# The causal mask and the exponential of a chunked state-space scan, set up on another engine

## The chip, the cores and the metric

The kernel is one launch on one core of a Trainium2 chip. The metric is the device time of that launch in microseconds (us). The version before takes 2398.5 us, the median of three runs (2398.19 to 2401.05).

## The reference, cut to what matters

One layer of a decoder, 1024 tokens wide and long: sparse attention beside a Mamba-2 scan, gated and merged, then a squared-ReLU MLP. The change lies in the scan, in the part that works within chunks of 128 tokens:

```python
a_cum = jnp.cumsum(dt * a, axis=2)                    # within a chunk of 128 tokens, per head
seg = a_t[..., :, None] - a_t[..., None, :]           # a_cum[l] - a_cum[s]
decay = jnp.exp(jnp.where(tril, seg, -jnp.inf))       # 0 where s > l
cb = jnp.einsum('bclgn,bcsgn->bcgls', cm, bm)
y_diag = jnp.einsum('bcgls,bcghls,bcsghp->bclghp', cb, decay, xdt)
```

There are 4 groups of 8 heads and 8 chunks, so the 128x128 matrix `cb` is made 32 times and `decay` (8 heads of 128x128) 32 times.

## The kernel before, in words

Every engine has its own program, in a fixed order written by hand; they meet only at semaphores. TensorE (PE) carries the big products. Each float32 operand is split into a high and a low part, so a product is three matmuls. GpSimd (POOL) splits the weights, SyncE (SP) loads them.

The scan runs group by group (`for g in range(NG)`), in the profile from about 831 us to 1305 us. The four groups begin their chunk loops near 831, 967, 1097 and 1228 us. In a group the function `segments(k)` on PE prepares chunk k. It makes `cb` in PSUM bank 7 (`mm(ps[:, 7, 0:P], b_fm, c_fm)`, two records), and then, for the 8 heads, eight "pick" matmuls of 128 columns in bf16. A pick takes one head's row of `a_cum` out of `seg_rows`, in three bf16 pieces, and spreads it over 128 partitions in banks 0 and 1. So bank 0 and 1 hold a_cum[l] for partition s and column l.

ScalarE (ACT) turns that into the decay. Eight instructions (L1502) compute relu(a_cum[s] - a_cum[l]), with `dta` as the copy of a_cum with its sign kept; one more of 1024 columns (L1506) computes exp(-that). The relu keeps the exponent from growing where s > l; it does not zero that half. VectorE (DVE) does: L1905 copies `cb` out of PSUM times the 0/1 triangle `tri` into `cb_sb`, and L1908 multiplies the eight 128x128 decay matrices by it, in place. PE then uses them as weights (`ps<-xdt,decay`).

`decay` has two buffers, `cb_sb` and the banks 0, 1 and 7 one each. PE's program in a group is: segments(0), a part of "fill" work, segments(1), another part, and then for k = 0 to 7: the products of chunk k (wait for `mix_ready` of chunk k), segments(k + 2), and some fill. Fill is an independent projection (the z of the next group, or in the last group a gate) that is cut into parts of 24 matmuls of 256 columns, or 12 of 512 in the last group; one or two such parts stand in an iteration, none in the last two of the last group. segments(k) waits twice: before `cb` for `cb_out` of chunk k - 1, which tells that bank 7 has been read, and before the picks for `decay_done` of chunk k - 1, which tells that banks 0 and 1 have been read. On DVE, `mix_in(k + 1)` (L1905 and L1908) stands ahead of the state and output steps of chunk k (L1922 to L1937), the last of which signals `y_ready`. On ACT, each chunk's decay is followed by `fill_evac` (L1382) and `squares_of` (L1490).

Ahead of the first chunk of a group ACT still copies out the last transposed tile (L1444).

Of the kernel before, what the change touches and what calls it, by code (L numbers as in the profile page):

```python
# [14 lines left out]
P = 128  # L15
F32 = mybir.dt.float32
F32R = mybir.dt.float32r
BF16 = mybir.dt.bfloat16
ALU = mybir.AluOpType
# [41 lines left out]
def hybrid_block(nc, x, c, ada_w, ada_b, norm_g, w_in, kv_norm_g, kidx_norm_g, w_uk, w_uv, conv_w, conv_b,  # L61
# [6 lines left out]
    NS = dt_bias.shape[1]  # L68
# [74 lines left out]
    tri = place("tri", [P, P], F32)  # L143
    future = place("future", [P, P], F32)
    vec_a = place("vec_a", [P, 112], F32)
    vec_b = place("vec_b", [P, 112], F32)
# [107 lines left out]
    with ctx:  # L254
# [291 lines left out]
        def _(pool):  # L546
            nc.gpsimd.memset(ones[:, :], 1.0).then_inc(const_made, 1)
            nc.gpsimd.memset(ident[:, :], 0.0).then_inc(const_made, 1)
            nc.gpsimd.memset(future[:, :], 0.0).then_inc(const_made, 1)
            pool.wait_ge(const_made, 3)  # L550

# [7 lines left out]
                                    base=0, pattern=[[-1, P]], channel_multiplier=1).then_inc(const_made, 1)  # L559
            pool.wait_ge(const_made, 6)  # L560
            nc.gpsimd.tensor_copy(ident_bf[:, :], ident[:, :]).then_inc(const_made, 1)
# [78 lines left out]
        def _(pe):  # L640
# [59 lines left out]

            pe.wait_ge(const_made, 7)
            pe.wait_ge(small_in, 16 * 6)
# [265 lines left out]
            for g in range(NG):  # L968
# [57 lines left out]
                def segments(k):  # L1026


                    if k >= 1:
                        pe.wait_ge(cb_out, g * NT + k)  # L1030
                    r = slice(k * P, k * P + P)
                    mm(ps[:, 7, 0:P], b_fm[:, r], c_fm[:, r], start=True, stop=True)
                    if k >= 1:
                        pe.wait_ge(decay_done, 2 * (g * NT + k) - 1)
                    i0 = k % 4 * HG
                    for j in range(2):
                        o = ps[:, j, :]
                        for h in range(4):
                            last = mm(o[:, h * P:(h + 1) * P],
                                      seg_pick[0:NR, i0 + 4 * j + h:i0 + 4 * j + h + 1].broadcast_to([NR, P]),  # L1040
                                      seg_rows[0:NR, 2 * g + k // 4, :], start=(h == 0), stop=(h == 3))
                    last.then_inc(seg_done, 1)
# [42 lines left out]

            pe.wait_ge(decay_done, 2 * NG * NT)
            pe.wait_ge(fill_out, NG * 8)
# [100 lines left out]
        def _(act):  # L1188
# [156 lines left out]
            nc.scalar.activation(acum[:, :, :].rearrange(flat), ps[:, 6, 0:NT * NS], ACT.Copy, scale=-1.0).then_inc(aend_out, 1)  # L1345
            nc.scalar.copy(dta[:, :, :].rearrange(flat), ps[:, 6, 0:NT * NS]).then_inc(aend_out, 1)
            nc.scalar.activation(ea[:, :, :].rearrange(flat), ps[:, 6, 0:NT * NS], ACT.Exp).then_inc(aend_out, 1)
# [55 lines left out]
            for g in range(NG):  # L1403
# [92 lines left out]
                for k in range(NT + 2):  # L1496
                    if k < NT:
                        act.wait_ge(seg_done, g * NT + (k + 1))
                        if k >= 2:
                            act.wait_ge(mix_done, g * NT + (k - 1))  # L1500
                        for h in range(HG):
                            ins = nc.scalar.activation(decay[k % 2][:, h, :], ps[:, h // 4, (h % 4) * P:(h % 4 + 1) * P], ACT.Relu,  # L1502
                                                       bias=dta[:, k, bass.ds(g * HG + h, 1)], scale=-1.0)
                        ins.then_inc(decay_done, 1)
                        act.wait_ge(decay_done, 2 * (g * NT + k) + 1)
                        nc.scalar.activation(decay[k % 2][:, :, :], decay[k % 2][:, :, :], ACT.Exp, scale=-1.0).then_inc(decay_done, 1)  # L1506
                    if k == 1:
                        fill_evac(g, 1 if g else 0)
                    for part in fill_parts(g, k - 2) if k >= 2 else ():
                        if part % 2:  # L1510
                            fill_evac(g, part // 2)
                    if g == NG - 1 and k >= NT - 1:
                        first_acts({NT - 1: (0, 1), NT: (2,), NT + 1: (3,)}[k])
                    if k >= 2:
                        squares_of(k - 2)
# [121 lines left out]
        def _(dve):  # L1637
# [184 lines left out]
            dve.wait_ge(last_spilled, 16 * 2)  # L1822
            dve.wait_ge(aend_out, 4)
            V.link(ve.tensor_tensor(dte[:, :, :].rearrange("p c h -> p (c h)"), ps[:, 7, 0:NT * NS],
# [44 lines left out]
            for g in range(NG):  # L1869
# [30 lines left out]
                def mix_in(k):  # L1900

                    dve.wait_ge(seg_done, g * NT + (k + 1))
                    if g or k:
                        dve.wait_ge(mix_ready, g * NT + k)
                    ve.tensor_tensor(cb_sb[:, :], ps[:, 7, 0:P], tri[:, :], ALU.mult).then_inc(cb_out, 1)  # L1905
                    dve.wait_ge(cb_out, g * NT + (k + 1))
                    dve.wait_ge(decay_done, 2 * (g * NT + k + 1))
                    ve.tensor_tensor(decay[k % 2][:, :, :], decay[k % 2][:, :, :],  # L1908
                                     cb_sb[:, :].rearrange("p (o l) -> p o l", o=1).broadcast_to([P, HG, P]), ALU.mult).then_inc(mix_ready, 1)
# [188 lines left out]
```

## Time and profile before

| | |
|---|---|
| median of three runs | 2398.5 us |
| the profiled execution, its own time | 2398.5 us |
| its span | 2396.6 us |
| PE busy | 2315.8 us (97%) |
| DVE busy | 1336.9 us (56%) |
| ACT busy | 751.0 us (31%) |
| POOL busy | 960.2 us (40%) |
| chain that ended last, by engine | PE 89%, DVE 6%, issue 2%, ACT 2% |

The span is 1.9 us shorter than the time of the same execution. In a row of the profile, L and a number is the line of the kernel (nearly all matmuls have L648, the helper's line), `out<-in` are the tensors, and `[idle before <-releaser]` says how long the engine stood still and what ended it. PE's records overlap, since matmuls are pipelined: the distance between two starts is what one costs.

### The profile page before, as it was taken

The page shows a single profiled execution, that of the slowest core. Times are in us where ns is not written, and L with a number is a line of the kernel's source. Part 1 is how long each engine was busy: PE and PEld are TensorE (multiplying, and loading weights), DVE is VectorE, ACT ScalarE, POOL GpSimd, SP SyncE. Part 2 cuts the span into 40 slices and gives each one's busy share as a digit, 9 for nine tenths or more (in the row PEclk, how much of TensorE's full clock was granted, in tenths as well). Part 3 has the DMA queues.
Part 4 walks back from the last instruction along what each step waited for, and adds up shares of the span by engine and source line. Part 5 has one row for each costly group of instructions (what it writes and reads, how often), then busy time and mean ns, then how long its engine had stood idle before and what let it go on. Part 6 is the DMA issues. An engine that isn't in the chain of part 4 may idle for free.

```text
span 2396.6 us, 31872 instructions
## 1 busy us (share of the span) xinstructions
PE 2315.8 (97%) x11958; PEld 1913.6 (80%) x11958; DVE 1336.9 (56%) x1988; ACT 751.0 (31%) x1363; POOL 960.2 (40%) x628
## 2 busy tenths in 40 slices
PE   3999999998999999999999999999999999999997
PEld 3977888885557998989887888899888888888886
DVE  4259999996657177685867545425522322322325
ACT  5144121005653244545466111025511112112112
POOL 1221333236672373654555334446333233233222
PEclk8999999999999999999999999999999999999999
DMA  7111452225652113141223354224211111111103
GB/s 276 36 36 39 147 189 90 88 97 163 209 164 80 36 63 132 45 145 45 86 104 140 141 176 141 99 95 167 80 48 41 53 53 35 53 53 43 45 35 79
DMA packets 144731, 230.28 MB, mean 96 GB/s; under 512 B 7956, under 2 KB 111732, under 8 KB 143604
## 3 DMA queue, kind: packets, MB, share of 16 engines
q1 hardware_dynamic: 119936, 166.11, 21.0%
q10 hardware_dynamic: 23684, 59.06, 6.4%
q0 software_dynamic: 1008, 3.67, 0.9%
q8 instruction: 73, 1.20, 0.2%
q14 instruction: 30, 0.25, 0.0%
HBM read 176.39 MB, written 52.43 MB: 95 GB/s over the span
## 4 chain that ended last, share of the span: by engine, by line
PE 89%; DVE 6%; issue 2%; ACT 2%; DMA 1%; ACTq 0%; DVEq 0%
PE ps L648 87%; DVE score L1731 2%; DVE probT L1814 1%; DVE mod_sum L1658 1%; PE ps L977 1%; PE ps L873 1%; PE ps L910 1%; DMA gate_d<-last_spill 0%; PE ps L696 0%; DMA acts_d<-decay 0%; ACT decay L1502 0%; DMA rows_b<-in_ssm_norm_g_dram 0%; DVE a_lo L1867 0%; DVE prob L1797 0%; DVE acc L1958 0%
## 5 line engine op out<-in xcount | busy, mean ns | idle before, releaser
L648 PE MATMUL ps<-a_hi,w_hi 128*128 128x512 f32 x1728 | 676.9, 392 | 2.0 <-DVE a_lo L1867 1.2
L648 PE MATMUL ps<-a_lo,w_hi 128*128 128x512 f32 x1728 | 672.8, 389 | 0.0
L576 POOL CAST w_hi<-raw 128x2048 fp32r<-128x2048 f32 x90 | 174.7, 1941 | 1180.6 <-issue 858.8
L648 PE MATMUL ps<-a_hi,w_lo 128*128 128x512 f32 x1728 | 543.0, 389 | 0.0
L580 POOL TENSOR_TENSOR w_lo<-raw,w_hi 128x512 fp32r<-128x512 f32 (+1 forms) x360 | 521.1, 1479 | 7.2
L2028 DVE TENSOR_TENSOR x_tm<-x_tm,ps 128x1024 f32<-128x1024 f32 x120 | 146.6, 1221 | 453.7 <-PE ps L648 453.1
L648 PEld LDWEIGHTS ps<-a_hi,w_hi 128*128 128x128 f32 x1728 | 324.5, 188 | 70.5 <-DVE a_lo L1867 2.0
L648 PEld LDWEIGHTS ps<-a_hi,w_lo 128*128 128x128 f32 x1728 | 324.4, 188 | 67.9
L648 PEld LDWEIGHTS ps<-a_lo,w_hi 128*128 128x128 f32 x1728 | 324.5, 188 | 66.2 <-issue 0.2
L648 PE MATMUL ps<-w_hi,a_hi 128*128 128x256 f32 (+1 forms) x896 | 259.2, 289 | 4.4 <-DVE a_lo L1867 2.7
L648 PE MATMUL ps<-w_lo,a_hi 128*128 128x256 f32 (+1 forms) x896 | 253.5, 283 | 0.0
L648 PE MATMUL ps<-w_hi,a_lo 128*128 128x256 f32 (+1 forms) x896 | 253.5, 283 | 0.0
L648 PE MATMUL ps<-w_lo,u_hi 128*128 128x512 f32 x512 | 204.3, 399 | 0.0
L1613 ACT ACTIVATE u_tmp<-ps 128x512 f32<-128x512 f32 x64 | 38.0, 594 | 522.7 <-PE ps L648 522.7
L648 PE MATMUL ps<-w_hi,u_hi 128*128 128x512 f32 x512 | 201.7, 394 | 0.0
L648 PE MATMUL ps<-w_hi,u_lo 128*128 128x512 f32 x512 | 200.7, 392 | 0.0
L648 PEld LDWEIGHTS ps<-w_hi,a_hi 128*128 128x128 f32 x896 | 172.4, 192 | 6.5 <-DVE a_lo L1867 2.9
L648 PEld LDWEIGHTS ps<-w_lo,a_hi 128*128 128x128 f32 x896 | 172.6, 193 | 1.5 <-issue 1.4
L648 PEld LDWEIGHTS ps<-w_hi,a_lo 128*128 128x128 f32 x896 | 172.4, 192 | 0.0
L1781 DVE MATCH_REPLACE8 score<-top,score 128x384 f32<-128x384 f32 (+2 forms) x192 | 171.3, 924 | 0.0
L1777 DVE MAX8 top<-score 128x8 f32<-128x384 f32 (+2 forms) x192 | 165.5, 926 | 0.0
L648 PEld LDWEIGHTS ps<-w_hi,u_hi 128*128 128x128 f32 x512 | 96.1, 188 | 25.0
(253 smaller groups left out, 3047.3 us busy)
## 6 DMA issues: line engine op xcount, KB each, us to landing
raw<-in_w_in_dram SPq DMA_DIRECT2D x35, 1024.0 KB, 5.1
ada_raw<-in_ada_w_dram SPq DMA_DIRECT2D x16, 1024.0 KB, 8.7
raw<-in_w_up_dram SPq DMA_DIRECT2D x16, 1024.0 KB, 5.4
raw<-in_w_down_dram SPq DMA_DIRECT2D x16, 1024.0 KB, 4.7
gates<-gate_d SPq DMA_DIRECT2D x12, 1024.0 KB, 4.9
act_raw<-acts_d ACTq DMA_DIRECT2D x20, 512.0 KB, 5.5
ada<-in_ada_w_dram SPq DMA_DIRECT2D x8, 1024.0 KB, 20.6
acts_d<-decay ACTq DMA_DIRECT2D x16, 512.0 KB, 4.4
```

The source lines that it names most:

```text
L576: nc.gpsimd.tensor_copy(hi, src).then_inc(hi_made, 1)
L580: nc.gpsimd.tensor_tensor(lo[:, c], src[:, c], hi[:, c].bitcast(F32), ALU.subtract).then_inc(w_split[s], 1)
L648: return nc.tensor.matmul(o, a, b, start=start, stop=stop)
L873: ins = nc.tensor.transpose(ps[:, 4 + turns % 2, (k % 4) * P:(k % 4 + 1) * P], prob[(t - 3) % 4][:, k * P:(k + 1) * P], ident[:, :])
L910: last = nc.tensor.transpose(ps[:, y_banks(g, f) + t // 4, (t % 4) * P:(t % 4 + 1) * P], zy[:, t, f * P:(f + 1) * P], ident[:, :])
L977: last = nc.tensor.transpose(ps[:, T_BANK[r] + t // 4, (t % 4) * P:(t % 4 + 1) * P], src[:, t * P:(t + 1) * P], ident[:, :])
L1613: nc.scalar.activation(u_tmp[j][:, :], ps[:, banks[j], :], ACT.Relu).then_inc(up_out, 1)
L1658: V.link(ve.scalar_tensor_tensor(mod_sum[:, :], ada0[:, k, :], c_act[:, k:k + 1], mod_sum[:, :], ALU.mult, ALU.add))
L1731: ins = ve.scalar_tensor_tensor(s, r, w, s, ALU.mult, ALU.add)
L1777: ve.max(top8[j][:, :], pair[j]).then_inc(topk_step, 1)
L1781: ve.match_replace(pair[j], top8[j][:, :], pair[j], TAKEN).then_inc(topk_step, 1)
L2028: ins = ve.tensor_copy(o, part) if first else ve.tensor_tensor(o, o, part, ALU.add)
```

## The change

The mask moves into the exponent. A constant `past_bf` (bf16) holds -1e30 where s > l and 0 elsewhere. In `segments` a matmul of 512 columns with the identity as weights lays it into bank 0 and into bank 1, four heads wide, and the picks accumulate onto it. ACT then needs one function: exp(bank + bias) with `acum`, the negated copy of a_cum, as bias, eight instructions of 128 columns. The pass over 1024 columns is gone, and so is `dta`'s refill. The copy of `cb` out of PSUM, now without the triangle, moves from DVE to ACT, ahead of the eight. So `cb_out` comes from ACT, and there ACT first waits for `mix_ready` of the chunk before, because `cb_sb` is single. `decay_done` is signalled once for a chunk, after the exponentials, where before it was signalled after the relus and after the exponential.

```diff
+    past_bf = place("past_bf", [P, P], BF16)
...
+            nc.gpsimd.memset(past_bf[:, :], 0.0).then_inc(const_made, 1)
+            nc.gpsimd.affine_select(out=past_bf[:, :], in_=past_bf[:, :], compare_op=ALU.is_ge, fill=NEG,
+                                    base=0, pattern=[[1, P]], channel_multiplier=-1).then_inc(const_made, 1)
...
@@ PE, segments(k)
                     if k >= 1:
-                        pe.wait_ge(decay_done, 2 * (g * NT + k) - 1)
+                        pe.wait_ge(decay_done, g * NT + k)
                     for j in range(2):
                         o = ps[:, j, :]
+                        mm(o.rearrange("p (h l) -> p h l", h=4), ident_bf[:, :],
+                           past_bf[:, :].rearrange("p (o l) -> p o l", o=1).broadcast_to([P, 4, P]), start=True)
                         for h in range(4):
                             last = mm(o[:, h * P:(h + 1) * P],
                                       seg_pick[0:NR, i0 + 4 * j + h:i0 + 4 * j + h + 1].broadcast_to([NR, P]),
-                                      seg_rows[0:NR, 2 * g + k // 4, :], start=(h == 0), stop=(h == 3))
+                                      seg_rows[0:NR, 2 * g + k // 4, :], stop=(h == 3))
@@ ACT
-            nc.scalar.copy(dta[:, :, :].rearrange(flat), ps[:, 6, 0:NT * NS]).then_inc(aend_out, 1)
...
                         act.wait_ge(seg_done, g * NT + (k + 1))
+                        if k >= 1:
+                            act.wait_ge(mix_ready, g * NT + k)
+                        nc.scalar.copy(cb_sb[:, :], ps[:, 7, 0:P]).then_inc(cb_out, 1)
                         if k >= 2:
                             act.wait_ge(mix_done, g * NT + (k - 1))
                         for h in range(HG):
-                            ins = nc.scalar.activation(decay[k % 2][:, h, :], ps[:, h // 4, (h % 4) * P:(h % 4 + 1) * P], ACT.Relu,
-                                                       bias=dta[:, k, bass.ds(g * HG + h, 1)], scale=-1.0)
+                            ins = nc.scalar.activation(decay[k % 2][:, h, :], ps[:, h // 4, (h % 4) * P:(h % 4 + 1) * P], ACT.Exp,
+                                                       bias=acum[:, k, bass.ds(g * HG + h, 1)])
                         ins.then_inc(decay_done, 1)
-                        act.wait_ge(decay_done, 2 * (g * NT + k) + 1)
-                        nc.scalar.activation(decay[k % 2][:, :, :], decay[k % 2][:, :, :], ACT.Exp, scale=-1.0).then_inc(decay_done, 1)
@@ DVE, mix_in(k)
-                    dve.wait_ge(seg_done, g * NT + (k + 1))
-                    if g or k:
-                        dve.wait_ge(mix_ready, g * NT + k)
-                    ve.tensor_tensor(cb_sb[:, :], ps[:, 7, 0:P], tri[:, :], ALU.mult).then_inc(cb_out, 1)
-                    dve.wait_ge(cb_out, g * NT + (k + 1))
-                    dve.wait_ge(decay_done, 2 * (g * NT + k + 1))
+                    dve.wait_ge(decay_done, g * NT + (k + 1))
                     ve.tensor_tensor(decay[k % 2][:, :, :], decay[k % 2][:, :, :],
                                      cb_sb[:, :].rearrange("p (o l) -> p o l", o=1).broadcast_to([P, HG, P]), ALU.mult).then_inc(mix_ready, 1)
```

On PE, at segments(1) of the first group (first fence before, second after), `seg_rows,seg_pick` are the picks and `w_hi`, `w_lo` rows are fill:

```order
L648 MATMUL ps<-w_hi_51,a_lo 128x256
L648 MATMUL ps<-c_fm,b_fm 128x128 [waits cb_out]
L648 MATMUL ps<-seg_rows,seg_pick 128x128 [waits decay_done]
L648 MATMUL ps<-seg_rows,seg_pick 128x128 x7
L648 MATMUL ps<-w_hi_51,a_hi 128x256
```

And the same place in the changed kernel:

```order
L652 MATMUL ps<-w_hi_51,a_lo 128x256
L652 MATMUL ps<-c_fm,b_fm 128x128 [waits cb_out]
L652 MATMUL ps<-past_bf,ident_bf 128x512 [waits decay_done]
L652 MATMUL ps<-seg_rows,seg_pick 128x128 x4
L652 MATMUL ps<-past_bf,ident_bf 128x512
L652 MATMUL ps<-seg_rows,seg_pick 128x128 x4
L652 MATMUL ps<-w_hi_51,a_hi 128x256
```

Two matmuls of 512 columns have come in, and the wait for `decay_done` now stands before the first of them.

On ACT, at the first two chunks of the first group, before (`xs_tm` is the last tile copied out, `c_in` the fill's evacuation):

```order
L1444 COPY xs_tm<-ps 128x8x128 [waits tile_turned]
L1502 ACTIVATE decay_140<-ps,dta 128x128 [waits seg_done,att_stored]
L1502 ACTIVATE decay_140<-ps,dta 128x128 x7
L1506 ACT_TABLE_LOAD
L1506 ACTIVATE decay_140<-decay_140 128x1024 [waits decay_done]
L1502 ACTIVATE decay_141<-ps,dta 128x128 [waits seg_done]
L1502 ACTIVATE decay_141<-ps,dta 128x128 x7
L1506 ACTIVATE decay_141<-decay_141 128x1024 [waits decay_done]
L1382 ACTIVATE c_in_133<-ps 128x512 [waits conv_done,fill_done]
```

And after:

```order
L1449 COPY xs_tm<-ps 128x8x128 [waits tile_turned]
L1506 COPY cb_sb<-ps 128x128 [waits seg_done,att_stored]
L1510 ACT_TABLE_LOAD
L1510 ACTIVATE decay_141<-ps,acum 128x128 x8
L1506 COPY cb_sb<-ps 128x128 [waits mix_ready,seg_done]
L1510 ACTIVATE decay_142<-ps,acum 128x128 x8
L1387 ACTIVATE c_in_134<-ps 128x512 [waits conv_done,fill_done]
```

The table load stood behind the eight instructions that free banks 0 and 1; it now stands ahead of them, as does the copy. There are as many table loads as before.

## Rows read from the trace of the kernel before

**Rows 1.** The page: busy time, share and instructions of three engines.

```profile
PE 2315.8 (97%) x11958; PEld 1913.6 (80%) x11958; DVE 1336.9 (56%) x1988; ACT 751.0 (31%) x1363; POOL 960.2 (40%) x628
```

**Rows 2.** Stretch, length; busy us of PE, PEld, DVE, ACT, POOL; clock, DMA, GB/s.

```profile
831.00:906.00 75.00, 75.00 (x600) 68.55 (x599) 49.82 (x56) 36.93 (x95) 49.79 (x34) 1.00 0.17 54
965.00:1040.00 75.00, 74.62 (x590) 67.56 (x589) 53.13 (x60) 37.47 (x96) 49.76 (x34) 1.00 0.17 54
1097.00:1170.00 73.00, 72.49 (x572) 65.38 (x571) 52.87 (x60) 36.47 (x95) 49.65 (x34) 1.00 0.17 55
1227.00:1305.00 78.00, 77.16 (x434) 61.67 (x432) 54.20 (x62) 59.45 (x114) 49.76 (x34) 1.00 0.23 82
```

**Rows 3.** PE in order of time, group 1: start, us, instruction.

```profile
966.90 0.61 PE L648 MATMUL ps<-seg_rows,seg_pick 96*128 96x128 bf16 x8
967.32 0.36 PE L648 MATMUL ps<-w_hi,a_hi 128*128 128x256 f32 x1
...
970.48 0.61 PE L648 MATMUL ps<-seg_rows,seg_pick 96*128 96x128 bf16 x8
...
973.95 1.97 PE L648 MATMUL ps<-xdt,decay 128*128 128x64 f32 x16
975.76 1.08 PE L648 MATMUL ps<-xde,b_tm 128*128 128x512 f32 x2
...
996.85 0.61 PE L648 MATMUL ps<-seg_rows,seg_pick 96*128 96x128 bf16 x8
```

**Rows 4.** PE, matmuls of 512 columns elsewhere in group 1.

```profile
950.59 0.39 PE L648 MATMUL ps<-a_hi,w_hi 128*128 128x512 f32 x1
950.82 0.39 PE L648 MATMUL ps<-a_lo,w_hi 128*128 128x512 f32 x1
...
984.87 1.08 PE L648 MATMUL ps<-state,c_fm 128*128 128x512 f32 x2
```

**Rows 5.** ACT in order of time, start of group 1.

```profile
967.05 1.01 ACT L1444 COPY xs_tm<-ps 128x1024 f32<-128x1024 f32 x1 [0.46 <-PE ps L977]
967.97 2.18 ACT L1502 ACTIVATE decay<-ps,dta 128x128 f32<-128x128 f32 x8
970.17 1.28 ACT L1506 ACT_TABLE_LOAD   x1
971.46 1.06 ACT L1506 ACTIVATE decay<-decay 128x1024 f32<-128x1024 f32 x1
972.43 2.16 ACT L1502 ACTIVATE decay<-ps,dta 128x128 f32<-128x128 f32 x8
```

**Rows 6.** ACT, two neighbours of equal shape, in the attention stage.

```profile
552.48 0.35 ACT L1346 COPY dta<-ps 128x256 f32<-128x256 f32 x1
552.74 0.38 ACT L1347 ACTIVATE ea<-ps 128x256 f32<-128x256 f32 x1
```

**Rows 7.** DVE in order of time, group 1.

```profile
972.62 1.23 DVE L1908 TENSOR_TENSOR decay<-decay,cb_sb 128x1024 f32<-128x1024 f32 x1 [4.23 <-ACT decay L1506]
...
992.35 0.28 DVE L1905 TENSOR_TENSOR cb_sb<-ps,tri 128x128 f32<-128x128 f32 x1
992.66 1.75 DVE L1908 TENSOR_TENSOR decay<-decay,cb_sb 128x1024 f32<-128x1024 f32 x1
```

**Rows 8.** ACT, start of group 3, the last.

```profile
1229.75 2.18 ACT L1502 ACTIVATE decay<-ps,dta 128x128 f32<-128x128 f32 x8
```

**Rows 9.** PE in order of time, start of group 3.

```profile
1231.98 0.62 PE L648 MATMUL ps<-seg_rows,seg_pick 96*128 96x128 bf16 x8 [0.26 <-ACT decay L1502]
...
1235.73 1.97 PE L648 MATMUL ps<-xdt,decay 128*128 128x64 f32 x16 [0.30 <-issue]
```

**Rows 10.** PE and what it waited for from 832 to 1350 us: total, times, longest.

```profile
PE ps L648 <- DVE a_lo L1867: 1.2, 1, 1.2
...
PE ps L648 <- DVE zy L1937: 0.8, 2, 0.4
```

**Rows 11.** PE's first instruction of the program.

```profile
9.11 0.42 PE L703 MATMUL ps<-ident,rows_a 112*128 112x112 f32 x1 [9.11 <-DMA rows_b<-in_ssm_norm_g_dram]
```

More of the change, by code:

```diff
@@ L549, in _ @@
             nc.gpsimd.memset(future[:, :], 0.0).then_inc(const_made, 1)
-            pool.wait_ge(const_made, 3)
+            nc.gpsimd.memset(past_bf[:, :], 0.0).then_inc(const_made, 1)
+            pool.wait_ge(const_made, 4)
             nc.gpsimd.affine_select(out=ident[:, :], in_=ident[:, :], compare_op=ALU.not_equal, fill=1.0,
@@ L559, in _ @@
                                     base=0, pattern=[[-1, P]], channel_multiplier=1).then_inc(const_made, 1)
-            pool.wait_ge(const_made, 6)
+            nc.gpsimd.affine_select(out=past_bf[:, :], in_=past_bf[:, :], compare_op=ALU.is_ge, fill=NEG,
+                                    base=0, pattern=[[1, P]], channel_multiplier=-1).then_inc(const_made, 1)
+            pool.wait_ge(const_made, 8)
             nc.gpsimd.tensor_copy(ident_bf[:, :], ident[:, :]).then_inc(const_made, 1)
@@ L698, in norm_turn @@
                     last.then_inc(turned, 1)
-            pe.wait_ge(const_made, 7)
+            pe.wait_ge(const_made, 9)
             pe.wait_ge(small_in, 16 * 6)
@@ L1084, in out_block @@
                 last.then_inc(w_used[n % 2], 1)
-            pe.wait_ge(decay_done, 2 * NG * NT)
+            pe.wait_ge(decay_done, NG * NT)
             pe.wait_ge(fill_out, NG * 8)
@@ L1822, in _ @@
             dve.wait_ge(last_spilled, 16 * 2)
-            dve.wait_ge(aend_out, 4)
+            dve.wait_ge(aend_out, 3)
             V.link(ve.tensor_tensor(dte[:, :, :].rearrange("p c h -> p (c h)"), ps[:, 7, 0:NT * NS],
```

## The prediction

> **What bounds the kernel now.** I read the page's busy times first. PE is busy for 97% of the span, DVE for 56%, ACT for 31% [rows 1]. Busy shares are averages, so I then read the stretches in which the change works. In windows of 73 to 78 us over the four groups' chunk loops, PE is idle for 0, 0.38, 0.51 and 0.84 us, at a granted clock of 1.00, which is the 2.4 GHz level [rows 2]. DVE is busy there for some 53 us of 75 and ACT for 37, in the last group 59 of 78. The waits of PE from 832 to 1350 us say the same: two waits of 0.8 us in total for `zy` (the signal `y_ready`), one of 1.2 us for `a_lo` after the scan [rows 10]. So in this stage every microsecond of added PE work is added to the end, and what ACT and DVE save is worth at most what PE waits for them, some 3 us in all. After the scan PE goes on with dense work of the same kind, so nothing gives a delay back.
>
> **What is added on PE: 64 mask matmuls.** Two per chunk, 32 chunks. Each streams 512 columns of bf16. The trace has no bf16 matmul of 512 columns. The nearest rows are the eight picks, which are bf16 and in the same place: from their first start to the first fill matmul it takes 967.32 - 966.90 = 0.42 us for 8 times 128 columns [rows 3], 0.0525 us each, or 0.21 us for 512. At 2.4 GHz, one column a cycle, it would be 0.213 us. The split-float32 matmuls of 512 columns start 0.23 us apart (950.82 - 950.59) [rows 4]. A plain float32 product of 512 columns is two records in 1.08 us [rows 3, 4], at most 0.54 each; that is the far upper end, 35 us for 64. Below, the cheapest matmul of the stage, 64 columns, takes (975.76 - 973.95) / 16 = 0.113 us [rows 3], which gives 7.2 us; a gain is excluded, since the matmuls are issued one after another on an engine that has no idle time to hide them in. I take 0.213, nearest to the picks: 64 x 0.213 = **13.7 us**. With 0.23 it would be 14.7.
>
> The Trainium skill, TensorE: Matmul & The Clock Gate, section on the back-to-back issue gap, gives two figures for 512 columns: about 216 ns for an isolated pair, and about 131 ns in a real stream of weight loads and matmuls. By the first, an estimate for the 64 is 13.8 us, by the second 8.4 us. The rows speak for the first: no pair of 512 columns here starts closer than 0.23 us [rows 4].
>
> The weights of the mask matmul, the identity, are loaded in the shadow of what goes before, as the picks' are. The change between 128-row float32, 96-row bf16 and back costs nothing that shows: 0.42 us is already 1024 columns at 2.4 GHz [rows 3].
>
> **What is added as a wait: segments(1) of each group.** Picks may overwrite banks 0 and 1 once ACT has read them. Before, that was at the end of the eight relus. In group 1 these run from 967.97 for 2.18 us [rows 5], to 970.15, and PE's second set of picks starts at 970.48 [rows 3]: just in time. Now ACT does, from the same start: the copy of `cb`, the table load of 1.28 us, and eight exponentials. The copy has no row of its own; one of the eight relus of 128 columns costs 2.18 / 8 = 0.27 us in a row [rows 5], and that is what I take, with 0.35 (a lone copy of twice the width [rows 6]) as the upper and 0 as the lower end. An exponential costs what a relu does: copy and exponential of equal shape are 0.35 and 0.38 us long, 0.26 apart [rows 6]. Sum 0.27 + 1.28 + 2.18 = 3.73 us. ACT was held until 967.97 by the tile copy [rows 5], and segments(0) now ends 0.43 us later (two masks), at about 967.94, so the start stays. The exponentials end at 971.7 and PE can go on at 971.75. PE gets there at 970.48 + 0.43 = 970.91. **Stall 0.84 us** in group 1, and the same by the same pattern in groups 0 and 2.
>
> In group 3, ACT starts its eight only at 1229.75 [rows 8], because a sigmoid and its table stand ahead of them; PE already waits, and its picks start at 1231.98 [rows 9]. Now the exponentials end at 1229.75 + 3.73 = 1233.48, the mask starts at 1233.53 and the picks at 1233.96, 1.98 us later than before, of which 0.86 are masks, so 1.1 are new wait. But the products of chunk 0 started late too, at 1235.73, waiting for DVE's product, about 0.45 us past PE's arrival (the row shows 0.30) [rows 9], and a third fill part waits 0.3 us for ACT; both are covered now. Net about **0.4 us**.
>
> In the other chunks the wait is hidden. segments(k + 2) is followed by at least one fill part (some 3 us, 967.32 to 970.48 with the next `cb`) and the next chunk's products (2.8 us, 973.95 to the end of the row at 975.76) before the next picks want banks 0 and 1 [rows 3]: some 5.8 us against 0.05 + 0.27 + 2.18 = 2.5 us, or 3.8 with a table load in group 3.
>
> **The added wait of ACT for `mix_ready`.** Queued behind it on ACT are the copy of `cb`, the exponentials, the fill evacuation and the squares. DVE's product of chunk k + 1 stands ahead of the state steps of chunk k, and at 992.66 + 1.75 = 994.4 it is done [rows 7], while the next picks only start at 996.85 [rows 3], so ACT does not wait for it. It waits at chunk 1: chunk 0's product ends at 971.7 + 0.1 + 1.23 [rows 7] = 973.0, about when the picks of chunk 1 end (971.75 + 0.86 = 972.6, and the last one drains some 0.2 us later). The exponentials of chunk 1 then end at 975.5; PE, which comes to the products of chunk 0 at 973.95 + 0.86 + 0.84 less what it waited, 975.6, wants banks 0 and 1 again 2.8 us after that. Nothing there.
>
> **What goes.** On DVE 0.28 us per chunk [rows 7], on ACT 1.06 - 0.27 = about 0.8 us (the pass over 1024 columns [rows 5] less the copy). Both are beside PE. What they and the masks give back are waits: the start of chunk 0's products in groups 1 and 2 (the product ends at 972.62 + 1.23 = 973.85 [rows 7], PE starts at 973.95 [rows 3]), 0.09 us each; and the two waits for `y_ready`, 0.8 us [rows 10], which fall in iterations with one fill part, where DVE's chain is as long as PE's and PE now has 0.43 us more to do. Together **-1.0 us**, at most -2.
>
> **Edits that cost nothing.** Two more POOL instructions at the start end long before PE's first at 9.11 us, which waits for a DMA [rows 11]. The refill of `dta` on ACT, 0.26 us [rows 6], stands beside attention work bound elsewhere.
>
> **The sum**, against the profiled execution, whose time (2398.5) is the median of the runs: 2398.5 + 13.7 + 3 x 0.84 + 0.4 - 1.0 = **2414 us**.
>
> **The rivals.**
> A: the table load costs more than its row. The Trainium skill, ScalarE: Activation LUTs, section "What ACT_TABLE_LOAD costs", adds a drain of about 1.4 us to each load of about 1.28 us; by that, an estimate for the four places is 5.5 us more. As a mechanism of this kernel: the load would have to wait until the copy ahead of it has left the pipe. The rows are against more than a trifle: load, 970.17 to 971.45, follows the relus' end at 970.15, and the exponential starts at 971.46 [rows 5]. If ACT lost one more load's length, 1.28 us, at each of the four starts, the time would be 2414 + 5.1 = 2419 us. Chance 5%.
> B: the masks cost less than a column a cycle, down to 0.113 us [rows 3]. 7.2 in place of 13.7 gives 2407.5 us. Chance 5%.
> C: DVE becomes the bound in iterations with one fill part, because its product runs at 1.75 us or more when POOL works beside it, and ACT, now serial with it through `cb_sb`, hands over late. For it speaks that PE already waits there; against it that ACT's path is 0.8 us shorter and PE's 0.43 longer. Price: some 0.5 us in each of 12 such iterations, 6 us, 2420 us. It decides where DVE's chain is over 7.6 us. Chance 5%.
> D, the other side: the relief of DVE and ACT wins. It needs PE to be bound by them in the chunk loop, with the masks falling into waits. It decides from the point where PE's waits exceed 13.7 us; the rows show 1.7 us in the four windows [rows 2]. Its price is all waits of the stage taken away, at most 3 us, and masks in the shadow: 2395.5 us. Chance 3%.
> E: the change does not do what it says, for instance the masks are not issued one by one. The order of instructions shows two per chunk; 2%, with no change, 2398.5.
>
> **How the numbers follow.** Forecast 80%: its own spread is 13.4 to 14.7 for the masks, 1.5 to 5 for the waits, -2 to 0 for what is given back, so 2411.5 to 2418. A and C push the upper end to 2420, B the lower to 2409. About 0.2% (4.8 us) is what can be told from no change. Slower by more: forecast, A, B, C, 95%; within: 2%; faster: 3%.
>
> **What the profile after would show.** 64 rows of `past_bf,ident_bf`, each start 0.21 us before the next pick; PE busy up by about 13.7 us while the waits in the stage stay under 6 us. At segments(1) of groups 0, 1 and 2 an idle of about 0.8 us of PE, released by ACT's exponentials, 1.5 to 2 us in group 3. ACT without waits for DVE except at chunk 1. The two waits for `zy` gone. It is wrong if a mask's distance is well off 0.21, or if PE waits for ACT or DVE in the middle of a group.

## The result, and the profile after

The changed kernel takes 2412.2 us (median of five runs, 2411.5 to 2413.6) against 2398.2 us (five runs, 2397.4 to 2401.1) for the one before: ratio 1.0059, 95% interval 1.0046 to 1.0073. It is 13.9 us slower; +15.5 was forecast. The profiled execution took 2412.2 us with a span of 2410.4, 13.8 us more than before.

The page's busy times, to be read against [rows 1]:

```profile
PE 2327.9 (97%) x12022; PEld 1919.5 (80%) x12022; DVE 1328.8 (55%) x1956; ACT 723.3 (30%) x1362; POOL 953.3 (40%) x630
```

DVE lost 8 us and ACT 28 us, PE got 64 instructions and 12.1 us more. The engine that bounds the kernel got the work. The four chunk loops, in the columns of [rows 2], each window moved along with its group:

```profile
829.00:906.00 77.00, 76.24 (x597) 67.85 (x596) 45.73 (x45) 30.00 (x94) 47.99 (x34) 1.00 0.16 52
968.00:1043.00 75.00, 74.12 (x579) 65.61 (x579) 47.60 (x48) 30.38 (x94) 48.08 (x34) 1.00 0.16 54
1103.00:1177.00 74.00, 73.12 (x570) 64.61 (x570) 47.27 (x48) 29.57 (x94) 48.08 (x34) 1.00 0.17 55
1237.00:1316.00 79.00, 77.25 (x439) 61.04 (x438) 49.58 (x49) 52.11 (x112) 47.52 (x34) 1.00 0.21 76
```

PE's idle time went from 0, 0.38, 0.51 and 0.84 us to 0.76, 0.88, 0.88 and 1.75, at the same granted clock of 1.00. Where it stands idle is seen in PE's rows of group 1 (start, length, instruction, idle before it), against [rows 3]:

```profile
970.00 0.39 PE L652 MATMUL ps<-c_fm,b_fm 128*128 128x128 f32 x2
970.22 0.38 PE L652 MATMUL ps<-past_bf,ident_bf 128*128 128x512 bf16 x1
970.44 0.39 PE L652 MATMUL ps<-seg_rows,seg_pick 96*128 96x128 bf16 x4
970.66 0.38 PE L652 MATMUL ps<-past_bf,ident_bf 128*128 128x512 bf16 x1
970.88 0.39 PE L652 MATMUL ps<-seg_rows,seg_pick 96*128 96x128 bf16 x4
971.08 0.36 PE L652 MATMUL ps<-w_hi,a_hi 128*128 128x256 f32 x1
...
974.04 0.38 PE L652 MATMUL ps<-c_fm,b_fm 128*128 128x128 f32 x2
975.19 0.39 PE L652 MATMUL ps<-past_bf,ident_bf 128*128 128x512 bf16 x1 [0.77 <-ACT decay L1510]
...
979.01 1.89 PE L652 MATMUL ps<-xdt,decay 128*128 128x64 f32 x16
```

From the first mask to the first fill matmul it takes 971.08 - 970.22 = 0.86 us, where the eight picks alone took 0.42: 0.44 for two masks, 0.22 each. Then comes the new stall of segments(1). ACT's rows of the same place, against [rows 5], show what it waits for:

```profile
970.38 1.01 ACT L1449 COPY xs_tm<-ps 128x1024 f32<-128x1024 f32 x1 [0.46 <-PE ps L981]
971.39 0.27 ACT L1506 COPY cb_sb<-ps 128x128 f32<-128x128 f32 x1
971.67 1.28 ACT L1510 ACT_TABLE_LOAD   x1
972.96 2.17 ACT L1510 ACTIVATE decay<-ps,acum 128x128 f32<-128x128 f32 x8
977.00 0.27 ACT L1506 COPY cb_sb<-ps 128x128 f32<-128x128 f32 x1 [1.86 <-DVE decay L1909]
```

Copy, table load and eight exponentials, 0.27 + 1.28 + 2.17 us, end at 975.13, and PE's mask starts at 975.19. In the last group the same chain ends later (PE's rows, against [rows 9]):

```profile
1242.29 0.38 PE L652 MATMUL ps<-c_fm,b_fm 128*128 128x128 f32 x2
1244.43 0.39 PE L652 MATMUL ps<-past_bf,ident_bf 128*128 128x512 bf16 x1 [1.75 <-ACT decay L1510]
```

All waits of PE from 832 to 1365 us that the profile lists (what waits, for whom, us in total, times, longest), first after, then the three rows of before that [rows 10] leaves out or cuts off:

```profile
PE ps L652 <- ACT decay L1510: 4.1, 4, 1.8
PE ps L652 <- DVE a_lo L1873: 1.2, 1, 1.2
```

```profile
PE ps L910 <- ACT decay L1363: 0.9, 1, 0.9
...
PE ps L648 <- issue: 0.3, 1, 0.3
PE ps L648 <- ACT decay L1502: 0.3, 1, 0.3
```

So the sum of the waits went from 3.5 us (1.2 + 0.9 + 0.8 + 0.3 + 0.3) to 5.3: four new stalls, one in each group, 4.1 us, and 2.3 us of old waits gone.

Marks in the two traces say where the difference arose. The mark of a group is the start of its first `ps<-c_fm,b_fm`:

| piece | before, us | after, us | difference |
|---|---|---|---|
| start to group 0 | 831.30 | 830.24 | -1.1 |
| group 0 to group 1 | 135.38 | 139.76 | +4.4 |
| group 1 to group 2 | 130.44 | 134.29 | +3.9 |
| group 2 to group 3 | 130.38 | 134.08 | +3.7 |
| group 3 to the end | 1169.1 | 1172.0 | +2.9 |

From the scan's start on it is +14.9. The -1.1 ahead of it lies before any instruction of the scan that the change touches; the last section shows how much that start moves from profile to profile.

The steady chunk gives the cleanest number. In groups 0 to 2 the distance from one chunk's `ps<-c_fm,b_fm` to the next, where two fill parts stand, is 9.98 us before and 10.40 to 10.42 after: 0.43 for two masks, with no wait in it.

### The profile page after: what moved, and what is told of

It is laid out like the page before. It is cut to its first block, busy times and chain, and to the rows that moved or that the text cites. A ratio compares the mean times of both kernels' runs of the same rounds, so it can differ in the third digit from the quotient of the medians.

```text
span 2410.4 us, 31914 instructions
## 1 busy us (share of the span) xinstructions
PE 2327.9 (97%) x12022; PEld 1919.5 (80%) x12022; DVE 1328.8 (55%) x1956; ACT 723.3 (30%) x1362; POOL 953.3 (40%) x630
## 4 chain that ended last, share of the span: by engine, by line
PE 90%; DVE 5%; issue 2%; ACT 2%; DMA 1%; ACTq 0%; DVEq 0%
PE ps L652 88%; DVE score L1737 2%; DVE probT L1820 1%; DVE mod_sum L1664 1%; PE ps L877 1%; PE ps L914 1%; PE ps L981 1%; ACT decay L1510 0%; PE ps L700 0%; DMA gate_d<-last_spill 0%; DMA rows_b<-in_ssm_norm_g_dram 0%; ACT L1510 0%; DVE prob L1803 0%; DVE acc L1959 0%; DVE a_lo L1873 0%
```

## The experiments

Four medians of the kernel before stand behind them: 2398.2 to 2399.2 us.

**The masks alone, in the kernel before.** To the kernel before are added `past_bf` and, in `segments`:

```diff
+                        mm(o.rearrange("p (h l) -> p h l", h=4), ident_bf[:, :],
+                           past_bf[:, :].rearrange("p (o l) -> p o l", o=1).broadcast_to([P, 4, P]), start=True)
```

> The kernel before with the constant and the 64 mask matmuls added and nothing else (relu, exponential of 1024 columns, DVE's copy times the triangle all stay; the result is the same, the half above the diagonal comes out as exp of minus a huge number). Theory M: 64 x 0.22 = 14.1 us more, less the waits that PE's longer iterations cover (0.8 for y_ready, 0.5 to 0.8 in group 3, 0.2 in the others): 2398.2 + 12.3 to 13 = 2410.5 to 2411.2, and no wait for ACT above 0.3 us at segments(1). Rival W: under 2405. A rival by which masks cost 0.13 us each, as in a stream where weight loads and matmuls overlap: 2405.5.

2410.1 us (2406.2 to 2411.2, five runs), ratio 1.0048 [1.0034, 1.0061]: +11.8. PE's waits in the scan, beside the 1.2 us for `a_lo`:

```profile
...
PE ps L652 <- ACT decay L1508: 0.2, 1, 0.2
```

The old waits of 0.9, 0.8 and 0.3 us are no longer listed: 64 masks by 0.215 to 0.22 make 13.8 to 14.1 us, less 2.1, 11.7 to 12.0. The profiled execution was the fastest of the five, 2406.2 us; its scan began 3.4 us earlier than before's, and from there to the end it is 11.1 us longer. A steady chunk takes 10.41 us, as in the changed kernel. The masks carry most of the loss, and they alone cover the old waits; no relief of DVE or ACT is needed for it.

**The masks twice.** Each is issued a second time into the same bank:

```diff
+                        mm(o.rearrange("p (h l) -> p h l", h=4), ident_bf[:, :],
+                           past_bf[:, :].rearrange("p (o l) -> p o l", o=1).broadcast_to([P, 4, P]))
```

> The changed kernel with every mask matmul issued twice (the mask is then -2e30, its exponential 0 all the same). Theory M: another 64 x 0.22 = 14.1 us, and in groups 0 to 2 the wait at segments(1) does not shrink by the first set's extra, since ACT's start moves with the end of segments(0): 2412.2 + 14.1 + up to 0.4 x 2 = 2426 to 2427.5. If a mask that follows a mask with the same weights is cheaper (its weight load dropped), 0.213 in place of 0.22: 2425.8. Rival: a mask costs 0.13: 2420.5.

2426.9 us (2425.5 to 2427.2, four runs), ratio 1.0115 [1.0099, 1.013]: 14.7 us over the changed kernel, within what was expected. By time that is 0.23 us for each of 64 more, but the trace says 0.215: a steady chunk takes 10.84 us in place of 10.41. The rest is not the masks'. A piece of 528 matmuls in the MLP took 66.28 us against 65.11 in the changed kernel, at a granted clock of 0.50, the 1.2 GHz level, from 1609 to 1615 us.

**The changed kernel without the masks.**

```diff
-                        mm(o.rearrange("p (h l) -> p h l", h=4), ident_bf[:, :],
-                           past_bf[:, :].rearrange("p (o l) -> p o l", o=1).broadcast_to([P, 4, P]), start=True)
...
-                                      seg_rows[0:NR, 2 * g + k // 4, :], stop=(h == 3))
+                                      seg_rows[0:NR, 2 * g + k // 4, :], start=(h == 0), stop=(h == 3))
...
-                                                       bias=acum[:, k, bass.ds(g * HG + h, 1)])
+                                                       bias=dta[:, k, bass.ds(g * HG + h, 1)])
```

> The changed kernel without its 64 mask matmuls; everything else of it stays (this leaves the causal mask out of the scan, and the exponentials take dta as bias, so that they stay finite). Theory M (the loss is the streaming of 64 times 512 columns, 0.22 us each, on an engine without idle time): 64 x 0.22 = 14.1 us less than the changed kernel's 2412.2, but the two waits for y_ready in groups 1 and 2 return (+0.8) and PE reaches segments(1) 0.43 us sooner while ACT's start stays, so the four waits there grow by about 0.4 each in groups 0 to 2: 2399 to 2400.5, with the waits for ACT at about 1.2, 1.2, 1.2 and 2.2 us. Rival W (the waits for ACT that the later decay_done brings are most of the loss): less than 7 us would go, 2405 or more. Rival S (some other cost of the change, such as memory placement or instruction fetch): stays at 2408 or more.

2403.5 us (2400.9 to 2404.6, eleven runs), ratio 1.002 [1.0011, 1.0029]. That is 3 us above what was expected, a miss. PE's waits:

```profile
PE ps L652 <- ACT decay L1508: 5.0, 4, 1.8
PE ps L652 <- DVE a_lo L1871: 1.2, 1, 1.2
PE ps L652 <- DVE zy L1936: 0.7, 2, 0.4
PE ps L914 <- ACT decay L1366: 0.4, 1, 0.4
```

They total 7.3 us against 3.5 before, 3.8 more: PE comes to segments(1) 0.43 us earlier than with masks and waits longer there. By the medians it is 5.1 us slower than before. The profiled execution was the fastest of the eleven, at 2400.9. By it the masks are worth 11.3 us (span 2410.4 - 2399.1), by the medians 8.7, where 11.7 to 13.2 was expected. One part is in the trace. Behind the stall of 1.8 us in the last group PE ran from 1236 to 1240 us at a granted clock of 0.62 and then 0.52, with matmuls of 512 columns 0.43 us apart in place of 0.23; that is some 1.6 us, and neither the kernel before nor the changed one has it. It was spared a like stretch near 1590 us: its piece of 528 matmuls took 63.62 us where both others took 65.1. What made the other ten runs 0.9 to 3.7 us longer no trace shows. The sign is settled, though: the relief without the masks is still slower than the kernel before.

**segments(1) one fill part later, in the changed kernel.** This takes away what makes PE wait:

```diff
                 fill(g, j, 0)
-                segments(1)
                 fill(g, j, 1)
+                segments(1)
```

> The changed kernel with segments(1) of each group put behind the second fill part (2.9 us of work) in place of ahead of it. Theory M says that the four waits for ACT at segments(1), 0.76, 0.77, 0.77 and 1.75 us, are all that is lost beside the masks, and ACT is done 0.8 to 1.8 us after PE wants it, less than a fill part: they vanish, and the later chunk 1 is still in time (its product would end near 980.5 where the state product that waits for the chain behind it comes at 986.5). So 4.0 us less: 2408 to 2408.7. Rival L (chunk 1, later by some 2 us, makes DVE's chain late, and the wait only moves to the products of chunk 1): 2410.5 to 2413, with waits of PE for DVE in the second iteration of each group.

2408.2 us (2407.2 to 2408.9, five runs), ratio 1.0039 [1.0025, 1.0053], 4.0 us less than the changed kernel. Its waits of PE, beside the 1.2 us for `a_lo`:

```profile
...
PE ps L652 <- ACT c_in L1387: 0.3, 1, 0.3
```

The four waits for the exponentials, 4.1 us, are gone and the time fell by as much (4.1 - 0.3 = 3.8). So the stall at segments(1) is real time, and the trace accounts for it.

**The same swap in the kernel before.**

> The kernel before with segments(1) behind the second fill part, as a candidate that is faster than both. Theory M: in the kernel before, PE waits there only in group 3 (0.3 us at the picks, 0.3 to 0.5 at the products of chunk 0), so at most 0.9 us goes: 2397.5 to 2398.4, not to be told from before by time. If chunk 1's product, now 2.9 us later, comes too late for the products of chunk 1 or for DVE's chain, up to 1 us more: 2399.4.

2399.7 us (2397.3 to 2402.0, ten runs), ratio 1.0007 [0.9997, 1.0016]: no difference that can be told. Its waits of PE:

```profile
PE ps L648 <- ACT c_in L1382: 2.0, 4, 0.9
PE ps L910 <- ACT decay L1363: 1.4, 1, 1.4
PE ps L648 <- DVE a_lo L1867: 1.4, 2, 1.2
PE ps L648 <- issue: 0.8, 1, 0.8
PE ps L648 <- DVE zy L1937: 0.7, 2, 0.4
```

They total 6.3 us against 3.5. There was little to win (the 0.3 us for `decay`), and 2.0 us of a new wait for the fill's evacuation came in; the forecast of a small gain was wrong. In the changed kernel the same swap brought 0.3 us of that wait and took 4.1 away, so there it pays.

**The copy back on DVE.** In the changed kernel ACT's copy and its wait go, and `mix_in` gets:

```diff
+                    dve.wait_ge(seg_done, g * NT + (k + 1))
+                    if g or k:
+                        dve.wait_ge(mix_ready, g * NT + k)
+                    ve.tensor_copy(cb_sb[:, :], ps[:, 7, 0:P]).then_inc(cb_out, 1)
+                    dve.wait_ge(cb_out, g * NT + (k + 1))
```

> The changed kernel with the copy of cb out of PSUM given back to DVE (a plain copy, waits as in the kernel before) and ACT's wait for mix_ready gone. Theory M: the wait at segments(1) shrinks by the copy's 0.27 us (decay_done comes that much sooner), so PE's waits for ACT fall from 4.1 to about 3.0 us; DVE gets 0.28 us more per chunk, but the masks' 0.44 us of PE cover it, so no wait for y_ready returns: 2412.2 - 1.1 = 2411.1. Rival X (moving the copy off DVE is what saved the waits for y_ready, not the masks): 0.8 us of waits for zy come back, 2411.9.

2412.5 us (2411.7 to 2413.3, four runs), ratio 1.0061 [1.0044, 1.0078]. The waits moved as expected, the time not:

```profile
PE ps L652 <- ACT decay L1507: 3.1, 4, 1.6
```

PE's four stalls for ACT are shorter by 4 x 0.25 us, and no wait for `zy` came back though DVE had its 0.28 us per chunk again. So the masks, not the moved copy, covered those. From the scan's start to the end the trace is 0.9 us shorter than after the change; the medians, which carry differences of that size from elsewhere, don't show it.

**Two buffers for `cb`.** The second is `tri`, free in the changed kernel, and ACT's wait looks one chunk further back:

```diff
-    cb_sb = place("cb_sb", [P, P], F32, o + 6 * K)
+    cb_sb = [place("cb_sb0", [P, P], F32, o + 6 * K), tri]
...
-                        if k >= 1:
-                            act.wait_ge(mix_ready, g * NT + k)
+                        if k >= 2:
+                            act.wait_ge(mix_ready, g * NT + k - 1)
```

> The changed kernel with two buffers for cb (the second one in tri, which is free by then), so that ACT's copy waits for mix_ready of two chunks before. Theory M: the added wait costs PE nothing, 2412.2 within 0.5; in the trace ACT's wait for DVE at chunk 1 of each group (1.9 us) is gone and PE's four waits are as they were, 4.1 us. Rival Y (the serial chain through the one buffer delays the later chunks): 2410 or less.

2413.3 us (2412.8 to 2413.8, four runs), ratio 1.0063 [1.0047, 1.008], 1.2 us above the changed kernel, where nothing was expected. PE's waits in the scan are the same to 0.1 us as after the change, 4.1 and 1.2. In the profiled execution the scan started at 831.6 us against 830.2, and from there to the end it is 0.3 us shorter than after the change. So the added wait of ACT for `mix_ready` costs nothing that shows.

**The table load early.** An exponential of one column ahead of the tile copy, into a new place of 32 bytes, takes the load out of the way:

```diff
     past_bf = place("past_bf", [P, P], BF16)
+    spare = place("spare", [P, 8], F32)
...
+                def exp_table():
+                    nc.scalar.activation(spare[:, 0:1], ones[:, 0:1], ACT.Exp)
...
+                    exp_table()
                     tile_evac(4)
...
+                    if g + 1 < NG:
+                        exp_table()
                     fill_evac(g, 0)
```

> The changed kernel with a one-column exponential put into ACT's program ahead of the last tile copy in group 0 and ahead of the fill evacuation in groups 1 and 2, so that the load of the exponential's table stands there and not between the copy of cb and the exponentials. Theory M (the load of 1.28 us is on PE's path at the start of a group): ACT has 0.5 us free in group 0 and 1.4 us in groups 1 and 2 to take up 1.28 + about 0.2, so the exponentials end 0.3 us sooner in group 0 and 0.8 to 1.2 in groups 1 and 2: of the 0.76, 0.77 and 0.77 us of PE's wait some 0.4, 0.1 and 0.1 stay, 2412.2 - 1.6 = 2410.6. Rival Z (the wait comes from the eight exponentials, not the load): the waits stay at 0.7 and more, 2412.

2402.4 us (2401.2 to 2406.1, ten runs), ratio 1.0019 [1.0009, 1.0028]: 9.8 us less than the changed kernel, 8 us better than expected. The mechanism did what it should; ACT's rows of group 1:

```profile
968.25 1.28 ACT L1447 ACT_TABLE_LOAD   x1
...
971.60 0.27 ACT L1513 COPY cb_sb<-ps 128x128 f32<-128x128 f32 x1
971.76 2.19 ACT L1517 ACTIVATE decay<-ps,acum 128x128 f32<-128x128 f32 x8
```

The exponentials follow the copy at once, and PE's waits for them fell to the one in the last group:

```profile
PE ps L653 <- ACT decay L1517: 1.8, 1, 1.8
```

That is 2.3 us less than 4.1. The rest arose after the scan, where the edit does nothing but shift tensors. The chain that ended last has one long piece of PE in the MLP (start, length, engine, count). After the change, and here:

```profile
1718.37 678.72 PE ps L652 x2946
```

```profile
1715.14 671.22 PE ps L653 x2946
```

The same 2946 matmuls take 7.5 us less. Four more runs went to that.

**The shift alone.** In the kernel before, and then in the changed one, nothing but an unused place of 32 bytes ahead of `vec_a`:

```diff
+    spare = place("spare", [P, 8], F32)
     vec_a = place("vec_a", [P, 112], F32)
```

> The kernel before with one unused place of 32 bytes ahead of vec_a, so that everything placed behind it, the MLP's u_hi and u_lo among it, starts 32 bytes later; no instruction differs. In the version with the early table, which had such a place, the down products of the MLP (1536 matmuls, weights u_hi and u_lo) started 0.229 us apart where in all other kernels of this study it is 0.233, and the last long piece of PE took 671.2 us in place of 678.7. Theory U (u_hi and u_lo stood 32 bytes off a multiple of 64 bytes and stand on one now): 7.3 us less, 2391, with 671.2 us for the last piece. Rival T (it was the added table loads or something else on ACT in that version): 2398.4 and 678.7 us.

> The changed kernel with the 32 bytes and without the early table. Theory U: 2412.2 - 7.3 = 2404.9. The version with the early table took 2402.4, so the table's place alone is then worth 2 to 2.5 us, as theory M said for it (three waits of 0.77, 2.3 us, gone). Against the shifted kernel before it measures the change anew, with the MLP faster: +13.9.

In the kernel before 2391.0 us (2389.6 to 2392.8, eight runs), ratio 0.997 [0.996, 0.9981]; in the changed one 2406.0 us (2405.3 to 2406.6, seven runs), ratio 1.0028 [1.0017, 1.004]. The first beats both kernels. Their difference, 15.1 us, is the change measured again in another layout. The long piece is 671.24 us in both and was 678.73 in the kernel before; in the first:

```profile
1704.42 671.24 PE ps L649 x2946
```

Against the second, the early table load was worth 3.6 us by the medians. The two profiles show 2.3 of waits, and 1.5 in the piece of 528 matmuls, which follows a wait of 2.7 us for `a_lo`: 63.6 us against 65.1. PE ran the start of that piece at a granted clock of 1.00 with the early load (1594 to 1600 us) and of 0.50 without it (1598 to 1600 us). The kernel without masks, which has no early load, and the shifted kernel before also took 63.6, so that part is not the early load's doing as far as the traces tell.

**A shift of 64 bytes** (`[P, 16]` in place of `[P, 8]`), and **the MLP's weights alone shifted by 32**:

```diff
-    u_hi = [place(f"u_hi{i}", [P, 2, SEQ], F32R, R2 + 16 * i * K) for i in range(2)]
-    u_lo = [place(f"u_lo{i}", [P, 2, SEQ], F32R, R2 + (8 + 16 * i) * K) for i in range(2)]
+    u_hi = [place(f"u_hi{i}", [P, 2, SEQ], F32R, R2 - 32 + 16 * i * K) for i in range(2)]
+    u_lo = [place(f"u_lo{i}", [P, 2, SEQ], F32R, R2 - 32 + (8 + 16 * i) * K) for i in range(2)]
```

> The same with 64 bytes, so that u_hi and u_lo are again 32 bytes off a multiple of 64. Theory U: no change, 2398.4 and 678.7 us for the last piece. Rival V (it is the distance to some other tensor, or any displacement from where they were): 2391 or some other time.

> The kernel before with u_hi and u_lo alone moved, 32 bytes down, onto a multiple of 64. Theory U: as good as the shift of everything, 2391 and 671.2 us for the last piece. Rival (another tensor's place matters): 2398.4.

With 64 bytes 2398.5 us (2395.4 to 2400.0, ten runs), ratio 0.9996 [0.9987, 1.0005]: by time nothing, as expected, though the long piece was 678.05 us, 0.7 shorter. With `u_hi` and `u_lo` alone 2397.0 us (2395.4 to 2399.4, ten runs), ratio 0.9993 [0.9984, 1.0002], where 2391 was expected. Its long piece took 677.22 us, 1.5 us less of 7.5. The theory that the address of `u_hi` and `u_lo` alone decides falls. What is shown is that a shift by 32 bytes of all that is placed behind it takes 7.5 us off the MLP, and one by 64 takes 0.7. Which tensor, or which pair, must move is open.

## Why the prediction was right

**The bound.** PE bound the stage, and the work added to it stood in the time in full. The experiments agree: masks +11.8, twice the masks +14.7 more; relief of DVE and ACT, no gain.

**The masks, 64 x 0.213 = 13.7 us.** Measured by the distance of starts: 0.44 us for two in group 1. In the last group a whole chunk goes from one of these rows of PE to the next:

```profile
1260.90 0.38 PE L652 MATMUL ps<-c_fm,b_fm 128*128 128x128 f32 x2
...
1271.05 0.38 PE L652 MATMUL ps<-c_fm,b_fm 128*128 128x128 f32 x2
```

That is 10.15 us in place of 9.72 (1267.95 - 1258.23 in the trace of before), 0.43 for two. So 0.215 to 0.22 each, 13.8 to 14.1 us; the choice of the picks as nearest row held. By starts, each of the 64 is followed by the next matmul after 0.21 to 0.23 us. Of the Trainium skill's two figures (TensorE: Matmul & The Clock Gate, section on the back-to-back issue gap) the trace bears out the isolated pair, about 216 ns, and not the 131 ns of a stream: none of the 64 masks, each between other matmuls, came near it.

**The stalls, 0.84 us in each of groups 0 to 2.** The trace shows 0.76, 0.77 and 0.77 of idle. By starts it is 0.93 in group 1: the first mask of segments(1) would follow `ps<-c_fm,b_fm` by 0.22 (970.22 - 970.00), at 974.26, and starts at 975.19. ACT's chain was 3.72 us long, 3.73 as forecast. It began 0.1 us later, since the copy of `cb` starts only when the tile copy has ended (970.38 + 1.01 = 971.39), where the relu overlapped it by 0.09 us [rows 5].

**The last group, +0.4 net.** From the group's mark to the mask of segments(1) it takes 6.06 us (1244.43 - 1238.37); 6.03 was forecast (1233.53 - 1227.50). The net has to be read at the third fill part, since the prediction counted a wait of 0.3 us there among what is covered. From the group's mark to its first matmul it takes 13.48 us (1251.85 - 1238.37) in place of 11.91 (1239.41 - 1227.50): 1.57 more, of which six masks are 1.3. That leaves 0.3; 0.4 was forecast. A second gap of 0.3 us, ahead of the first fill part of the group, was there before (0.75 us from the picks of segments(0) to it, where 0.42 is usual) and is covered too.

**Given back, -1.0.** The waits for `zy` (0.8 us) are gone from the list, as was said, but two things are off. The reason was half wrong: the masks on PE cover them, and DVE's relief adds nothing (the copy put back on DVE brought none of them back). And they are not gone altogether. In the iterations with one fill part of groups 1 and 2, first before and then after:

```profile
1027.41 1.89 PE L648 MATMUL ps<-xdt,decay 128*128 128x64 f32 x16
1029.68 1.10 PE L648 MATMUL ps<-state,c_fm 128*128 128x512 f32 x2 [0.38 <-DVE zy L1937]
```

```profile
1027.33 1.89 PE L652 MATMUL ps<-xdt,decay 128*128 128x64 f32 x16
1029.33 1.10 PE L652 MATMUL ps<-state,c_fm 128*128 128x512 f32 x2
```

The distance of starts fell from 2.27 to 2.00 us, and elsewhere it is 1.73. So 0.27 of 0.54 us is left at each of the two places, too short for the list of waits; only twice the masks take it away. That is the wait "in the middle of a group" which the prediction named as a sign of being wrong, at 0.5 us in all.

Another 0.9 us came back that the prediction did not name: the wait of the `zy` transposition for ACT near 1346 us (`PE ps L910`), in a stretch that the prediction called dense. ACT there waits for a DMA that stores its buffer:

```profile
1344.92 1.11 ACT L1363 ACTIVATE decay<-ps,vec_b 128x1024 f32<-128x1024 f32 x1 [4.91 <-DMA acts_d<-decay]
```

That transfer, issued at 1336.42, took 8.42 us. After the change the same step of ACT, at 1356.86, waits for PE alone, so its transfer, issued at 1350.76, landed within 6.1 us. The wait is there in each profiled kernel without masks (0.9 to 1.4 us; 0.4 in the changed one without them); of those with masks only the one with twice the masks has one, 0.2 us. Why the transfer is quicker there was not tested.

So this term was the one mis-sized. By starts, what came back is 0.8 us of waits for `zy` (0.27 at each of the two places above, 0.29 at one more in group 2), 0.17 at chunk 0's products in each of groups 1 and 2 (0.09 was forecast), 0.9 at `PE ps L910` and 0.3 at the first fill part of the last group: 2.3 us, past the forecast's own end of 2.

**The sum.** In the prediction's terms: masks 13.8, stalls 3 x 0.93 = 2.8, the last group 0.3, given back 2.3, so 14.6 us. The stretch behind the last long piece of PE is 0.5 us longer after, which nothing here explains; that makes 15.1 against 14.9 read from the scan's start to the end. The last 1.1 us to the measured +13.8 is the earlier start of the scan, which the prediction could not know. The masks, the stalls and the last group came out within 0.3 us each; what is given back was 1.3 us too small. Without that chance start the forecast of +15.5 would have missed by 0.6 us; with it the miss is 1.6.

**What costs nothing.** The wait of ACT for `mix_ready`: it waits at chunk 1 as said (977.00, idle 1.86 us, released by DVE's product), later than forecast since that product took 1.67 us and not 1.23:

```profile
975.24 1.67 DVE L1909 TENSOR_TENSOR decay<-decay,cb_sb 128x1024 f32<-128x1024 f32 x1 [7.65 <-ACT decay L1510]
```

PE doesn't come for banks 0 and 1 until 981.87, and two buffers changed nothing in its waits.

**The rivals.** A, a dearer table load: the load starts where the copy ends (971.39 + 0.27 = 971.66, 971.67) and the exponential 0.01 us after it. It costs its row, 1.28 us. The Trainium skill (ScalarE: Activation LUTs, "What ACT_TABLE_LOAD costs") adds a drain of about 1.4 us; no row here shows one. B, cheaper masks: excluded by 0.22. C, DVE the bound: two places of 0.27 us are left, as above, less than before and far from 6 us. D, the relief wins: the changed kernel without masks is 5.1 us slower than before, and it waits more, not less. E: 64 mask rows are there:

```profile
L652 PE MATMUL ps<-past_bf,ident_bf x64: 379/381/390, 830.5 to 1302.1; 128*128 128x512 bf16 x64
```

Their length of 0.38 us is not their cost: the next matmul starts 0.22 us after, and that says what one costs.

## What to carry to other kernels

Before work is moved, read which engine has no idle time in that stretch: work put there costs its full length, and relief elsewhere is worth at most what that engine now waits for it, here some 2 us against 14. When a function behind a buffer's release moves ahead of it (here copy and table load), count the distance from the release to the next writer, at the start of each group too and not only in the steady loop. And when an edit gives more than its mechanism can, look for where the time went before believing it: a scratch tensor of 32 bytes gave three times what the idea did.

## What the runs showed of the hardware

**Where tensors lie changes the rate of TensorE.** Within the MLP's down products (weights `u_hi` and `u_lo`), three matmuls of 512 columns repeat. In the kernel before, four repetitions apart:

```profile
1999.89 0.39 PE L648 MATMUL ps<-w_hi,u_hi 128*128 128x512 f32 x1
...
2002.69 0.39 PE L648 MATMUL ps<-w_hi,u_hi 128*128 128x512 f32 x1
```

In the kernel with the early table load, where all that lies behind the 32 bytes is shifted, eleven repetitions apart:

```profile
1952.07 0.39 PE L653 MATMUL ps<-w_hi,u_hi 128*128 128x512 f32 x1
...
1959.62 0.39 PE L653 MATMUL ps<-w_hi,u_hi 128*128 128x512 f32 x1
```

That is 2.80 / 12 = 0.233 us for one, against 7.55 / 33 = 0.229, some 2% closer, at a granted clock of 1.00 in both. The kernel before has `u_hi` at a byte address that is 32 over a multiple of 64; the change moved it by 256 bytes, so both kernels lie alike and the comparison of them is fair. It was good luck: an added constant of 32 bytes would have turned the verdict of a smaller change. Why 32 bytes matter, and for which tensor, is open.

**The clock falls in different places in different profiles.** Each of the fourteen profiles has, behind its first 100 us, two to four stretches of a few microseconds in which the granted clock was 0.50, the 1.2 GHz level, and not 1.00, the 2.4 GHz level. They don't stand in the same places. Near 557 us, where PE had waited 2.4 to 4.0 us for the attention's statistics, the kernel before and the one with masks alone differ (the columns of [rows 2]):

```profile
557.00:562.00 5.00, 4.80 (x9) 2.59 (x10) 3.41 (x12) 3.28 (x6) 4.92 (x3) 0.50 0.42 131
```

```profile
557.00:562.00 5.00, 5.00 (x16) 2.32 (x15) 4.60 (x13) 4.69 (x9) 4.92 (x3) 1.00 0.38 124
```

After the change it was 0.66. The scan began at 831.3, 827.9 and 830.2 us in these three. Over all profiles the start goes with that clock, though not by it alone: 831.2 to 831.6 at 0.50 (four), 829.7 to 831.2 at 0.66 or 0.69 (eight), 827.9 at 1.00. The shifted kernel before, with 0.66, began at 831.8; it has one more slow stretch, from 806 to 812 us. Another such place is the wait of 2.7 us for `a_lo` near 1590: the 528 matmuls behind it took 63.6 us in three profiles, without a slow stretch, and 64.9 to 66.3 in the other eleven, with one. So one slow stretch there costs 1.3 to 2.7 us. No edit tested what brings the clock down; the wait of PE ahead of it was 2.7 us with and without it. It limits what single profiles say of edits worth 1 or 2 us, and is why the copy on DVE and the two buffers were judged by waits and not by time.
